# A two-layer encoder whose triangular inversions start from solved 8 by 8 blocks instead of doubling from 1

## The reference

```python
a_mat = jnp.where(strict, jnp.einsum('bnhid,bnhjd->bnhij', kb, kc) * decay, 0.0)
unit_lower = a_mat + jnp.eye(C, dtype=a_mat.dtype)
u = solve(unit_lower, vb)                       # triangular_solve, unit diagonal
w = solve(unit_lower, kb * jnp.exp(gc)[..., None])
...
state = (state * jnp.exp(g_last)[..., None]
         + jnp.einsum('bhcd,bhce->bhde', k_i * jnp.exp(g_last - g_i)[..., None], v_new))
```

## Time and profile before

| what | value |
|---|---|
| median of 3 runs | 2767.75 us (2765.85 to 2768.54) |
| the profiled execution | 2771.26 us, span 2769.4 us |
| busy: PE, PEld, DVE | 98%, 86%, 56% |
| busy: ACT, POOL | 47%, 4% |
| the eight groups together | 238.38 us of the span |

### The profile page before, as it was taken

How to read it: one execution, slowest core, us unless ns; L and a number is a source line. 1 busy time by engine, 2 the same in 40 slices (tenths; PEclk the granted TensorE clock), 3 DMA queues, 4 the chain that set the end, 5 groups by cost and what they waited for, 6 DMA issues and landing times.

```text
span 2769.4 us, 44546 instructions
## 1 busy us (share of the span) xinstructions
PE 2725.2 (98%) x18174; PEld 2393.0 (86%) x18174; DVE 1542.8 (56%) x2048; ACT 1312.0 (47%) x1798; POOL 119.9 (4%) x167
## 2 busy tenths in 40 slices
PE   8999999999999999999999999999999999999999
PEld 8999998888888888888898997888888888888887
DVE  5655466666555555555544665666665555455454
ACT  4544444555544535445444354335555444354453
POOL 0000043000000000000000000530000000000000
PEclk9999999999999999999999999999999999999999
DMA  7454500543555555555545562004445545555553
GB/s 281 181 184 159 182 33 32 213 172 143 184 201 184 190 191 189 190 183 186 193 175 201 188 220 95 2 2 160 175 140 195 192 173 197 183 191 191 183 194 140
DMA packets 67801, 461.71 MB, mean 167 GB/s; under 512 B 7023, under 2 KB 10223, under 8 KB 13084
## 3 DMA queue, kind: packets, MB, share of 16 engines
q1 hardware_dynamic: 63824, 449.47, 45.3%
q10 hardware_dynamic: 3500, 5.21, 0.6%
q0 software_dynamic: 288, 4.19, 0.4%
HBM read 456.73 MB, written 5.27 MB: 167 GB/s over the span
## 4 chain that ended last, share of the span: by engine, by line
PE 94%; DVE 3%; ACT 2%; issue 1%; DMA 0%; POOL 0%; DVEq 0%; ACTq 0%; POOLq 0%
PE bank L423 17%; PE bank L402 13%; PE bank L404 13%; PE bank L403 13%; PE bank L425 9%; PE bank L446 6%; PE bank L448 6%; PE bank L447 6%; PE bank L1199 1%; PE bank L1172 1%; PE bank L337 1%; PE bank L2477 1%; PE bank L561 0%; PE bank L505 0%; DVE split_lo L353 0%
## 5 line engine op out<-in xcount | busy, mean ns | idle before, releaser
L353 DVE TENSOR_TENSOR split_lo<-raw,split_hi 128x1024 fp32r<-128x1024 f32 x840 | 1019.9, 1224 | 943.1 <-ACT split_hi L346 942.7
L346 ACT ACTIVATE split_hi<-raw 128x1024 fp32r<-128x1024 f32 x840 | 881.4, 1059 | 1137.6 <-PE bank L404 554.9
L423 PE MATMUL bank<-hT,split_hi 128*128 128x512 f32 x2048 | 720.8, 397 | 5.4 <-issue 5.3
L425 PE MATMUL bank<-hT,split_lo 128*128 128x256 f32 x2048 | 574.4, 280 | 0.0
L423 PEld LDWEIGHTS bank<-hT,split_hi 128*128 128x128 f32 x2048 | 385.0, 188 | 93.4 <-DVE split_lo L353 1.1
L402 PE MATMUL bank<-split_hi,u_hi 128*128 128x512 f32 x1152 | 449.8, 390 | 0.0
L404 PE MATMUL bank<-split_hi,u_lo 128*128 128x512 f32 x1152 | 448.5, 389 | 0.0
L403 PE MATMUL bank<-split_lo,u_hi 128*128 128x512 f32 x1152 | 448.4, 389 | 0.0
L425 PEld LDWEIGHTS bank<-hT,split_lo 128*128 128x128 f32 x2048 | 387.4, 189 | 5.7 <-issue 5.6
L446 PE MATMUL bank<-hT,split_hi 128*128 128x256 f32 x1328 | 376.8, 284 | 0.0
L448 PE MATMUL bank<-hT,split_lo 128*128 128x256 f32 x1328 | 375.8, 283 | 0.0
(11 more groups left out here) (471 smaller groups left out, 2266.4 us busy)
## 6 DMA issues: line engine op xcount, KB each, us to landing
raw<-in_stream SPq DMA_DIRECT2D x420, 1024.0 KB, 4.8
work<-in_mem POOLq DMA_DIRECT2D x2, 2048.0 KB, 8.5
bias_rows<-bias_line SPq DMA_DIRECT2D x1, 3072.0 KB, 12.9
x<-in_x SPq DMA_DIRECT2D x1, 2048.0 KB, 9.0
out<-x SPq DMA_DIRECT2D x4, 512.0 KB, 4.9
mwork<-bias_rows ACTq DMA_DIRECT2D x1, 1536.0 KB, 11.2
work<-bias_rows ACTq DMA_DIRECT2D x1, 1536.0 KB, 10.1
rwork<-in_wide ACTq DMA_DIRECT2D x1, 1280.0 KB, 5.9
```

Source lines behind the costliest of these rows:

```text
L346: nc.scalar.activation(split_hi[:, u % SPLIT], raw[:, b % RAW, (u % 2) * UNIT:(u % 2 + 1) * UNIT], ACT.Copy).then_inc(s_hi, 1)
L353: nc.vector.tensor_tensor(split_lo[:, u % SPLIT], raw[:, b % RAW, (u % 2) * UNIT:(u % 2 + 1) * UNIT], f32(split_hi[:, u % SPLIT]), SUB).th ...
L423: nc.tensor.matmul(out[:, :], lhsT=w_hi[:, cols], rhs=hT[:, k].rearrange("p two s -> p (two s)"), start=k == 0, stop=False)
L425: m = nc.tensor.matmul(out[:, S:2 * S], lhsT=w_lo[:, cols], rhs=hT_hi[:, k, :], start=False, stop=k == KD - 1)
```

## The change

Levels 0, 1 and 2 of the doubling are gone (`BASE` = 3). In their place the 8 by 8 diagonal blocks are solved exactly. DVE gathers the blocks of one d by a masked product, a sum over blocks and a masked product (`dve_inv_blocks`). PE spreads each block over its own rows with one fp32 product of 512 columns with the constant `around` (`pe_inv_around`). DVE then solves all blocks of both directions together, column by column, by 14 dependent operations of 8 to 56 elements, and writes `T` and `Tt` with two masked products and two transposes (`dve_inv_solve`). This happens for the group behind, in slots of the group at hand. An inversion is now levels 3 to 6, with slots 0 to 15 on PE.

The slot tables are new. In the delta rule `cum`, `mask` and `kk` of direction 0 are prepared two groups ahead (slot 15), the squares of the output move from DVE to ACT, and A is made before QK. In RWKV the products `pairs` are split: `first` gives A alone (128 columns), and the rest comes later; `cum` is two groups ahead. There are 36 unread products instead of 16 ahead of the first RWKV inversion. The 4 and 5 (delta rule) or 4 and 7 (RWKV) at slots 20 and 23 give way to 8 at slot 15 of each inversion that has another behind it in its layer, and 7 and 10 in the first RWKV group become 7 and 7. POOL makes three masks fewer for each d.

```diff
+BASE = 3
+TINY = 1 << BASE
...
-            for level in range(1, LEVELS):
+            for level in range(BASE, LEVELS):
                 pe_inv_level(pe, group, views, AT, level, between)
...
-        def dve_inv_first(dve, group, views, d):
-            T, Tt, _, MT, _ = views
...
-            eye = const[:, C["eye"]].unsqueeze(1).broadcast_to([P, 4, HALF])
-            nc.vector.tensor_tensor(Tt[:, d], eye, MT[group * MASKS % len(MT)][:, d], SUB).then_inc(iv_tt, 1)
...
+        def dve_inv_blocks(dve, group, views, d):
+
+            T, Tt = views[0][:, d], views[1][:, d]
             if group >= 2 and d == 0:
                 dve.wait_ge(iv_f, group - 1)
...
+            dve.wait_ge(iv_a, 2 * group + d + 1)
+            own = const[:, C["blocks"]].unsqueeze(1).broadcast_to([P, 4, HALF])
+            dve_step(nc.vector.tensor_tensor(Tt, iv_diag[:, d], own, MULT))
+            dve_step(nc.vector.reduce_sum(tiny[:, 0, d], blocks_of(Tt).rearrange("p m b c -> p m c b"), AX_X))
...
+            nc.vector.tensor_tensor(blocks_of(T), got.broadcast_to(shape), unit.broadcast_to(shape), MULT).then_inc(iv_blk, 1)
+
+        def pe_inv_around(pe, group, views):
+
+            pe.wait_ge(iv_blk, 2 * group + 2)
...
+            nc.tensor.matmul(rep_bank(group)[:, :], lhsT=const[:, C["around"]],
+                             rhs=views[0].rearrange("p d m n -> p (d m n)"), start=True, stop=True).then_inc(iv_rep, 1)
+
+        def dve_inv_solve(dve, group, views):
...
+            dve.wait_ge(iv_rep, group + 1)
+            nc.vector.tensor_copy(row[:, :, 0:1], unit[:, :, 0:1])
...
+            for k in range(1, TINY - 1):
+                left = TINY - 1 - k
+                dve_step(nc.vector.tensor_tensor(part[:, :, 0:left], N[:, :, k, k + 1:],
+                                                 row[:, :, k:k + 1].broadcast_to([P, 8, left]), MULT))
+                dve_step(nc.vector.tensor_tensor(row[:, :, k + 1:], row[:, :, k + 1:], part[:, :, 0:left], SUB))
...
-        DN_PE = {'tail': (0, 1, 3, 7, 9), 'cum': (0, 13), 'mask': (2, 13), 'kk': (0,), 'kq': (10,)}
-        DN_ACT = {'tail': (0, 1, 3), 'pre': (1, 7), 'diag': (9, 11)}
-        DN_DVE = {'R': 1, 'out': 3, 'squares': 5, 'QKT': (5, 8), 'AT': (7, 9), 'first': (9, 11)}
+        DN_PE = {'tail': (0, 2, 4, 7, 10), 'cum': (15, 2), 'mask': (15, 2), 'kk': (15,), 'kq': (6,), 'around': 8}
+        DN_ACT = {'tail': (0, 1, 3), 'pre': (7, 1), 'diag': (1, 2), 'squares': 4}
+        DN_DVE = {'AT': (0, 1), 'blocks': (2, 2), 'R': 1, 'solve': 3, 'out': 5, 'QKT': (6, 7)}
...
+            elif (c, u) == (5, 4):
+                pe_inv_around(pe, 0, dn_inv[0])
...
+            pe_rwkv_cum(pe, 1)
+            pe_inv_around(pe, 4, rw_inv[0])
+            pe_fill(bank[3], 36)
...
-        RW_DVE = {'state': 1, 'out': 4, 'mean': 5, 'variance': 8, 'scales': 9, 'pre': (4, 5), 'pairs': (7, 7, 9, 9), 'first': (9, 11)}
-
-        RW_FIRST = {'keys': (1, 3, 3), 'bonus': (5, 11), 'bonus PE': 23}
...
+        RW_PE = {'tail': (0, 2, 4, 6, 7, 9), 'cum': 15, 'first': 5, 'around': 8, 'pairs': (11, 14)}
+        RW_ACT = {'tail': (0, 0, 1, 2, 3), 'pre': (0, 1), 'diag': (3, 3)}
+        RW_DVE = {'pre': (0, 1), 'state': 1, 'scales': 1, 'first': 2, 'blocks': 3, 'solve': 3, 'out': 4, 'pairs': (5, 7),
+                  'mean': 5, 'variance': 6}
+
+        RW_FIRST = {'keys': (0, 1, 1), 'bonus': (3, 7), 'bonus PE': 13}
```

More of the change, by code:

```diff
@@ L105 @@
 CONST_COLS = [
-    ("ident", P), ("level", 2 * (LEVELS - 1) * (P // 2)), ("eye", P // 2),
+    ("ident", P), ("level", 2 * (LEVELS - 1 - BASE) * (P // 2)),
+    ("blocks", P // 2), ("around", P), ("unit", TINY), ("unit_neg", 1),
     ("neg", 2 * P), ("cum_mid", 4 * P), ("causal", 4 * P), ("halves", P), ("ones", 1), ("half_cols", 2),
@@ L1179, in pe_inv_level @@
                 i.then_inc(iv_p, 1)
-                between(4 * level - 4 + d)
+                between(4 * (level - BASE) + d)
             for d in range(2):
@@ L1362, in pe_even @@
                 Gemm(pe, "ev_sc").column_chunk(c, after_unit=lambda u, c=c: pe_delta_head(pe, c, u))
+            for piece in ("cum", "mask", "kk"):
+                pe_delta_pre(pe, 1, 0, piece)
             for hp in range(DN_GROUPS):
                 def between(slot):
+                    if hp + 1 < DN_GROUPS and slot == DN_PE["around"]:
+                        pe_inv_around(pe, hp + 1, dn_inv[(hp + 1) % 2])
                     for step in range(5):
@@ L1479, in pe_delta_pre @@
                                          stop=piece == "cum" or i == 1)
-                m.then_inc(s_pre if piece == "cum" else s_mask, 1)
+                if piece == "mask":
+                    m.then_inc(s_mask, 1)
                 return
@@ new lines, in dve_rwkv_first @@
+        def dve_rwkv_first(dve, f):
+            for d in range(2):
+                for i in range(2):
+                    dve.wait_ge(s_rM, RW_EVENTS * f + 3 + i)
+                    mask = const_of("causal", 2 * d).unsqueeze(1).broadcast_to([P, 2, P])
+                    nc.vector.tensor_tensor(rAT[f % 2][:, d, 2 * i:2 * i + 2],
+                                            bank[2 + i][:, 2 * d * P:2 * (d + 1) * P].rearrange("p (t s) -> p t s", s=P),
+                                            mask, MULT).then_inc(s_rMAT, 1)
@@ L2575, in between @@
                 def between(slot):
+                    for d in range(2):
+                        if f + 1 < RW_F and slot == RW_ACT["pre"][d]:
+                            act_rwkv_pre(act, f + 1, d)
                     for step in range(5):
@@ L2680, in between @@
                             dve_rwkv_bonus(dve, step)
+                    for d in range(2):
+                        if f + 1 < RW_F and slot == RW_DVE["pre"][d]:
+                            dve_rwkv_pre(dve, f + 1, d)
                     if f and slot == RW_DVE["state"]:
                         dve_rwkv_state(dve, f - 1)
+                    if f == 0 and slot == 0:
+                        dve_rwkv_pairs(dve, 0, 1)
+                    if f + 1 < RW_F and slot == RW_DVE["scales"]:
+                        dve_rwkv_scales(dve, f + 1)
+                    if f + 1 < RW_F and slot == RW_DVE["first"]:
+                        dve_rwkv_first(dve, f + 1)
+                    for d in range(2):
+                        if f + 1 < RW_F and slot == RW_DVE["blocks"]:
+                            dve_inv_blocks(dve, 5 + f, rw_inv[(f + 1) % 2], d)
+                    if f + 1 < RW_F and slot == RW_DVE["solve"]:
+                        dve_inv_solve(dve, 5 + f, rw_inv[(f + 1) % 2])
                     if f and slot == RW_DVE["out"]:
@@ L2956, in constants @@
     c[:, at["level"]] = level.reshape(P, -1)
-    c[:, at["eye"]] = own == t_
+    c[:, at["blocks"]] = own // TINY == t_ // TINY
+    c[:, at["around"]] = s // TINY == t // TINY
+    c[:, at["unit"]] = s % TINY == np.arange(TINY)[None, :]
+    c[:, at["unit_neg"]] = -1.0 * (s % TINY == 0)
     c[:, at["neg"]] = np.where(np.hstack([s <= t, s >= t]), 0.0, NEG)
```

406 lines of the change are left out of this document (247 added, 159 removed).

## The result

The changed kernel takes 2840.32 us (median of 4 runs, 2822.79 to 2847.06) against 2768.14: a ratio of 1.0253, 95% interval 1.0203 to 1.0302. I had forecast 2781 and a range that ended at 2796. The direction was right, the size far too small: +72 us instead of +13. The profiled execution is the shortest of the four, 2822.79 us with a span of 2821.0; the others show a lower clock.

What follows compares the result with a forecast made beforehand. TensorE was taken to bound the kernel (94% of the chain). Delta rule -10.6, RWKV +13.4, clock +7 and shared access +3 gave +12.8 on the profiled 2771.26; against the median 2781 us, range 2754 to 2796.

Steps and rivals of the forecast that it cites:

- the price of the clock: New waits of 3 to 5 us bring half-clock stretches: +7 us (5 RWKV, 2 delta rule), ends 0 and 14.
- my walk: Engine orders priced group by group: delta rule -10.6 us, RWKV +13.4, first RWKV group 41 us against 31.66.
- ports: Blocks and solve beside POOL's masks slow down by shared access: +3 us, 0.5 in six groups, ends 0 and 6.
- The list of waits and their places: TensorE's new waits: 3.1 us at the delta rule's first around; 2.3, 3.7, 3.2, 5.4, 1.7 in first RWKV group.
- the signs that I had named: Clock under 0.9 in RWKV groups 0 and 1, first RWKV group 38 to 44 us, delta-rule groups 1 to 3 at 20 to 24.
- The solve's price: VectorE's 14 small operations plus two products and transposes take 4.65 us per group, ends 4.1 and 6.6.
- the work falls by 28 us: TensorE's products removed and added, all groups, sum to -28 us; as full as before, some 2743 us.
- Groups 1 and 2 of RWKV: Second and third RWKV groups: 36.7 us against 36.51 (+0.2) and 32.3 against 33.72 (-1.4).
- The delta rule's first group: Gains nothing since VectorE is its bound; TensorE waits 1.4 and 2.9 us: 21.9 against 21.33, +0.6.
- A: Rival: idle time as walked, but clock stays at 1.00 and ports don't clash: +2.8, about 2770 us; chance 0.20.
- B: Rival, faster: VectorE reaches blocks 4 us earlier in the first RWKV group, waits shrink, 2758 us; chance 0.28.
- C: Rival: the solve's small steps take 0.35 us each, 2 us per solve in six groups, clock 14: 2800 us; chance 0.07.

Runs made afterwards that it cites:

- Experiment 2: The changed kernel with 167 more unread products placed in TensorE's waits: 2810.7 us, ratio 1.0156 against the kernel before.
- Experiment 8: The kernel before without its unread products inside the inversions (90 products): 2786.4 us, ratio 1.0057.
- experiment 3: The changed kernel with GpSimd's masks of a group made only after VectorE has gathered both directions' blocks: 2820.2 us.
- experiment 5: The changed kernel with GpSimd's norm weights (two operations of 1024 columns per group) run behind the next RWKV group's masks: 2825.4 us.
- experiment 1: The changed kernel run again, nothing edited: 2833.37 us, ratio 1.0224 against the kernel before.
- combined kernel: The changed kernel with late masks, later first around, late norm weights, keys and bonus moved, fewer unread products in remaining waits, end ones before cum: 2801.5 us.
- experiment 12: The combined kernel with the solve's twelve small dependent operations left out (wrong inverse, only time read): 2791.1 us.
- experiment 13: The kernel before with eleven more unread products in and behind the first RWKV group's long wait and bonus, bonus products one slot earlier: 2762.4 us against 2768.5.

## Why the prediction was wrong

**The step that failed: the price of the clock.** The prediction said that each half-clock stretch "costs up to half its length where TensorE sets the pace, and nothing where it waits anyway", and took 7 us, 14 at most. Summed from the windows (length times what is missing to 1.00), the clock in RWKV's groups 0 to 2 missed 14.3 + 11.1 + 8.4 = 34 us in the best execution, where those of before missed 7. A part of it lies in time in which TensorE only waited. What it can have cost in TensorE's own time is half of the time that TensorE was busy at half clock. These are the stretches at half clock in the three groups, the third number being TensorE's busy time:

```profile
1777.73:1787.97 10.24, 6.36 (x56) 5.85 (x58) 8.18 (x22) 1.66 (x4) 2.94 (x4) 0.50 0.00 0
1791.38:1798.21 6.83, 3.10 (x24) 1.60 (x24) 4.42 (x12) 0.00 (x0) 0.85 (x1) 0.50 0.00 0
1805.03:1818.69 13.66, 11.08 (x63) 8.88 (x63) 2.87 (x7) 1.35 (x5) 0.00 (x0) 0.50 0.01 2
1828.93:1845.99 17.06, 11.45 (x89) 9.23 (x86) 9.28 (x27) 3.46 (x9) 5.18 (x7) 0.50 0.01 1
1859.65:1863.06 3.41, 3.08 (x7) 2.53 (x8) 0.27 (x1) 0.00 (x0) 0.00 (x0) 0.50 0.00 0
1876.71:1893.78 17.07, 11.46 (x91) 9.24 (x90) 8.67 (x24) 3.47 (x9) 4.92 (x6) 0.50 0.00 1
```

That is 46.5 us, of which half is 23; before it was 13.7 us (the two stretches of the earlier trace rows, to their full length), of which half is 7. Over the whole program TensorE was busy at half clock for 87.9 us, against 17.1 before. The halves differ by 35 us. So, as an estimate, the clock has up to 35 of the 51.6 us, where I had 7. I had taken for the length of such a stretch (6 to 7 us behind one wait), and forgot the next wait: in the first RWKV group three stretches at half clock (the last runs into the next group) have only 3.4 and 6.8 us at full clock between them. And "nothing where it waits anyway" is wrong in a chain: P, first, around and the pairs run ahead of what VectorE waits for, and at half clock they take longer (14 unread products 3.35 us for 1.83, around 2.07 for 1.12, cum 3.78 for 1.89). I had TensorE busy for about 25 us of the first RWKV group; it was 32.74, and these 7.7 us are most of the 10.1 by which the group missed my walk. Experiment 2 shows the clock's share: 23 us come back for more work. Experiment 8 shows it in the kernel before.

**The second: ports.** I took 3 us, 6 at most, for shared access from one row (937 against 426 ns), as 0.5 for each group. What decides is the length of GpSimd's operation, not of VectorE's: the factors of two groups lay beside operations of 1.9 and 2.4 us, and two of them took 4.7 us instead of 0.8. I looked at GpSimd's new order for what it waits on, and not for what VectorE has beside it. Blocks cost 4.4 us instead of 2.5 for both d ahead of the delta rule; 0.4 of it is the sum over 8 blocks, which takes 0.61 us without GpSimd too. Experiments 3 and 5 show both places; their sizes in the whole are within the scatter.

**What was right.** The list of waits and their places (chunk 5, first, level 4, around, cum) and their lengths in the first RWKV group: 2.3, 3.7, 3.2, 5.4 and 1.7 us walked, 1.92, 2.70, 3.97, 6.51 and 2.58 measured, 16.3 and 17.7 in sum. So the waits were right, and what they do to the clock was not. Of the signs that I had named, the clock under 0.9 in RWKV groups 0 and 1 came (0.72, 0.77); the first RWKV group at 38 to 44 us (51.2) and the second delta-rule group at 20 to 24 (26.9) did not. The solve's price, 4.65 against 4.74. Groups 2 and 3 of the delta rule kept their gain (-5.1 and -6.9 of -6.7 and -6.3), as did RWKV's last (-3.4 of -2.5). That the work falls by 28 us was counted from the instructions; it shows in TensorE's busy time only where the clock is 1.00: the third delta-rule group, 22.12 us against 27.74 before (which includes preparation that now lies in other groups).

**The terms mis-sized by hand.** Groups 1 and 2 of RWKV: walked +0.2 and -1.4, measured +11.9 and +8.5. Besides the clock the walk missed the wait at first (2.8 and 3.2 us, behind factors that lay beside GpSimd's long operations). The delta rule's first group came out at +6.0 for +0.6. Its idle time was as walked (4.3 us walked, 4.7 measured), but from 381.68 to 398.74 it ran at half clock, with TensorE busy for 14.2 us of that. The clock fell there 4 us ahead of around, shortly behind a wait of 1.71 us for ScalarE's copy of P (L1236).

**The rivals.** A (waits, but the clock stays at 1.00) is refuted by the granted clock of the changed profile (0.72, 0.77 and 0.80 in three groups), and its price by experiments 1 and 2. B (faster) asked for a first RWKV group under 38 us; it was 51. C (small steps at 0.35 us) is refuted by the changed kernel's profile, 0.17 to 0.27 each; beside GpSimd's masks single ones do reach 0.41 (experiment 3).

**What stays open.** The combined kernel keeps 33 us over the kernel before. Ten to thirteen are the solve's small operations (experiment 12). By place, half of it is the first RWKV group (46.8 us against 31.66), 7 us each are the way to the first P and the first delta-rule group (28.3 against 21.33), and the second and third delta-rule groups gain (3.6 and 5.2). The rest isn't split up by a run: blocks (2.9 us in each group, on the path wherever around waits), 20 more unread products ahead of RWKV (about 2.6 us of which lie behind the end of the solve), and VectorE's 30 us in the first group are what the profile offers. Nor is the cause of experiment 13's 6 us known. Nor did a run show why two executions of one program keep the clock in different groups.

## What to carry to other kernels

A program that runs at a clock of 1.00 because its waits are all covered has more to lose than the waits: price a new wait with half clock for what follows it, up to the next wait and beyond, and not once. A wait of 1.1 us stood in front of such a stretch in the earlier trace rows, one of 1.7 in the first delta-rule group after. Before moving an operation of VectorE or GpSimd, lay the two engines' orders side by side and look for what is long on GpSimd; the short one on VectorE pays the long one's time. Unread products in a wait are a cheap trial: a few lines gave 23 us back in the changed kernel, and without its own the kernel before is slower. Look also at where in the profile a gain lies before giving it a cause: that of experiment 13 lies mostly outside the part that was changed.

## What the runs showed of the hardware

- TensorE stayed at half clock while the profile shows it busy without a gap: 25.5 us at 0.51 (experiment 8), in a stretch of products of 32 to 128 columns. The Trainium skill, page "TensorE: Matmul & The Clock Gate", section "Part 1: The HAM clock gate", ties the clock to how busy TensorE has been; with the busy time of the profile this stretch doesn't agree, and the measurement stands. (The ends of matmuls are modelled in the profile, so short idle moments between them may not show.) In the changed kernel the clock fell to 0.51 after 8.9 us in which no gap was longer than 0.14 us:

```profile
422.60:426.00 3.40, 3.40 (x18) 3.40 (x17) 2.43 (x9) 1.03 (x3) 0.84 (x2) 0.51 0.01 2
```

- The same 8 unread products took 3.7 us there, and 2.0 at the end of the next inversion, at a clock of 1.00.
- A sum of 256 elements to 32 with a stride takes 0.61 us on VectorE, against 0.42 for a product of the same width.
- Operations of 8 to 56 elements took 0.16 to 0.27 us in the changed kernel, each waiting for the one before; in the solve at 1758 us they mostly started 0.21 to 0.25 us apart.
